# TensorE products without a reader, taken out of the norms of a three-block network

## The chip, the cores and the metric
One Trainium2 chip, one of its cores, one launch. The metric is device time in microseconds. The core has a matrix engine (TensorE, PE in the rows; its weight loads are PEld), VectorE (DVE), ScalarE (ACT), GpSimdE (POOL) and SyncE (SP), which here issues most DMAs. The engines run their own lists of instructions and meet through semaphores.

## The reference, cut to what matters
512 tokens with 1024 channels go through three blocks: a state-space and retention mixer with cross-attention and a gated feed-forward part; a gated convolution and recurrence with 128 experts chosen per token; and a mixer with gating, matrix memory and sparse attention, with a squared-relu feed-forward part. Between the parts stand norms over the 1024 channels, and they are what the change touches:

```python
def _layer_norm(x, g, b):
    mu = jnp.mean(xf, axis=-1, keepdims=True)
    var = jnp.mean(jnp.square(xf - mu), axis=-1, keepdims=True)
    return (xf - mu) * lax.rsqrt(var + EPS) * g + b
...
def third_block(x, c, ...):
        h = rms_norm_3(x, g_norm1[l]) * (1.0 + sc1) + sh1      # behind the second block's own rms norm
        x = x + gt1 * hybrid_mixer_3(h, ...)
        h = rms_norm_3(x, g_norm2[l]) * (1.0 + sc2) + sh2
        x = x + gt2 * (jnp.square(jax.nn.relu(h @ w_mlp1[l])) @ w_mlp2[l])
    return rms_norm_3(x, g_final)
```

## The kernel before, in words
Activations lie with the channel on the partitions: eight tiles of 128 channels x 512 tokens. A linear layer runs over output tiles of 128 channels; a tile takes, for each of the eight input tiles, three matmuls of 128x512 (high part of the weights by high part of the input, high by low, low by high; lines 1008 to 1010, in older form 758 to 760). ScalarE and GpSimdE or VectorE make the two parts of the weights from slabs that SyncE loads. In the rows a matmul on such rounded parts is one record, a matmul in full float32 is two.

A norm needs a sum over channels, that is across partitions, and TensorE makes it. The pieces of work are in `RowNorm`: `means` (line 1175, a 128x128 matrix of ones by the total of the eight tiles), `centre` on VectorE (1180), squares on ScalarE (1186), their sums on TensorE (1233, one row of 512; or 1222, eight matmuls with a single moving column), the root on ScalarE (1256 or 1258), in one form a turn of the row into columns (1240), the reciprocal on VectorE (1263 or 1266), `spreads` (1271: four 128x128 matmuls that bring the factors to all partitions), and then for each tile a scaling on VectorE (1279), the high part on ScalarE (1360, in one norm 1441) and the low part on VectorE (1369 or 1447). The next layer's matmuls wait for these tile by tile.

`Seam` places such a norm between two layers in each engine's list; its `on_pe` is what TensorE runs there. Five norms use the lines that change: the one behind the attention's output layer (`ln2`, line 2756), the one behind the first feed-forward part (`ln3`, 2757, as `WithoutRoot`, which inherits `on_pe`), the two norms in one between the second and the third block (`NormTwice`, 3550), the one ahead of the last feed-forward part (`normed`, 4389) and the final one (`final`, 4390). The norm `ln1` (2424) has a plan of its own that puts its pieces between real output tiles, and no products of this kind.

In between the pieces, `warm(pe, n)` issues n matmuls of a 128x128 matrix of ones with itself, into a PSUM bank that nobody reads at that time (bank 4, in `NormTwice` bank 7). They wait for nothing and signal nothing. The counts are 4, 4 and 6 in `ln2` and `ln3`; 4, 2 and 6 in `normed` and `final`; 3, 6 and 5 in `NormTwice`: 66 in all.

Of the kernel before, what the change touches and what calls it, by code (L numbers as in the profile page):

```python
# [22 lines left out]
P = 128  # L23
# [1261 lines left out]
class Seam:  # L1285
# [12 lines left out]
    def begin(self, split, made, round0):  # L1298
        self.split, self.made, self.round0 = split, (self.s.evac_done, made), round0

    def warm(self, pe, count):
        for _ in range(0 if self.pe_plan else count):
            pe.matmul(self.s.ps[4][:, 0:P], self.s.ones, self.s.ones, start=True, stop=True)  # L1303

    def add_made(self, dve, t):
        if self.first.center:
            self.first.add(dve, t, self.made)
        elif self.first.most_on_dve and t >= 2:
            self.first.add_early_square(dve, t - 1)
# [5 lines left out]
    def sum_up(self, pe, t):  # L1315
        if not self.first.center and not self.first.most_on_dve:
            self.first.column_of_square(pe, t)

    def on_pe(self, pe):
        x, y = self.first, self.second  # L1320
        self.warm(pe, 4)
        if x.center:
            x.means(pe)
            self.warm(pe, 4)
            yield
        if x.sums_on_dve:
            x.column_of_total(pe)
            yield
        elif x.most_on_dve:
            x.columns_of_early_squares(pe)  # L1330
            x.columns_of_last_square(pe)
            yield
        else:
            for t in range(0 if x.center else DT - 2, DT):
                x.column_of_square(pe, t)
                yield
        self.spread(pe, x)
        yield
        if y:
            for t in range(DT):  # L1340
                y.column_of_square(pe, t)
                yield
            self.spread(pe, y)
            yield

    def spread(self, pe, x):
        if x.by_rows:
            x.turn_row(pe)
        else:
            self.warm(pe, 2)  # L1350
        x.spreads(pe)
        self.warm(pe, 6)

    def high(self, act, k):
        x = self.last
# [193 lines left out]
class NormTwice(Seam):  # L1549
# [18 lines left out]
        self.sums = [s.ps[b][:, 0:2 * TT].rearrange("p (j n) -> p j n", n=2) for b in (5, 2)]  # L1568
        self.last = self

    def warm(self, pe, count):
        for _ in range(count):
            pe.matmul(self.s.ps[7][:, 0:P], self.s.ones, self.s.ones, start=True, stop=True)

    def sum_up(self, pe, t):
        pass

# [99 lines left out]
            self.scale(dve, 0, i - 46)  # L1677

    def on_pe(self, pe):
        self.warm(pe, 3)  # L1680
        for t in range(DT):
            self.sum_square(pe, 1, t)
        self.turn_rows(pe, 1)
        self.warm(pe, 6)
        self.spreads(pe, 1)
        self.warm(pe, 5)
        yield

    def shift(self, act, t):
# [108 lines left out]
def first_projection(s):  # L1798
# [79 lines left out]
    def warm(pe):  # L1878
# [8 lines left out]
        part("w_qk", x, store(lambda t: s.qk[:, t, :]), side=first_convs, side_steps=12, side_after="w_xbc"),  # L1887
        part("w_v", x, store_by_token(s.vt, TT), tokens=TT, pe_before=partners, side=rotate, evac_before=silu_beside),
    ], act_start=first_function, sync_first=lambda sync: load_start(s, sync), sync_last=load_rope, pool_end=next_low, pe_start=warm, input_there=input_there)
    s.loaded.passed(16)  # L1890
    s.tables_loaded.passed(16)
# [183 lines left out]
def state_space(s):  # L2075
# [59 lines left out]
    def on_pool(pool):  # L2135
        for _ in range(5):
            yield
        for h in range(SSD_HEADS):
            if h in (2, 12):
                yield  # L2140
            x.weigh_others(pool, h)

    linears_beside(s, [part("w_z", s.x_split, store(lambda t: s.sz[:, t, :]))], Beside(20, 1.0, on_pe, on_act, on_dve, lead=21, pool=on_pool))
    x.passed()

# [57 lines left out]
def retention(s):  # L2203
# [79 lines left out]
    def on_dve(dve):  # L2283
        step = Chain(dve, s.dve_chain)
        dve.wait_ge(s.loaded.sem, s.loaded.at(16))
        for n in range(TT * x.PAIRS):
# [7 lines left out]
            if n in (13, 15):  # L2294
                normalize(dve, step, (13, 15).index(n))

    linears_beside(s, [part("w_g", s.x_split, store(lambda t: s.sg[:, t, :], ACT.Silu))], Beside(18, 1.0, on_pe, on_act, on_dve, load_decay))
    s.loaded.passed(16)
    s.iota_loaded.passed(16)
# [5 lines left out]
def mix(s):  # L2305

    waiting, sq, std = s.view(0, 8), s.view(54, 2), s.arena[0:RET_HEADS, 56 * T:57 * T]
    mean_ready, cen_ready, sq_ready, var_ready, std_ready, spread, applied, high_ready = s.beside_sems[0:8]  # L2310
    y, heads = s.result, RET_HEADS
    mixed = Split(y, 8, s.rounded(8), s.rounded(37))
# [77 lines left out]
    def load_memory(sync):  # L2390
        sync.dma_start(flat(16), s.I["mem"]).then_inc(s.loaded.sem, 16)

    linears_beside(s, [part("w_mixu", Split(lambda k: s.u[:, k, :], 8, s.rounded(58), s.rounded(66)), store(lambda t: waiting[:, t, :]))],
                   Beside(20, 0.95, on_pe, on_act, on_dve, load_memory, lead=8))
    for c, n in ((mean_ready, 8), (cen_ready, 8), (sq_ready, 8), (var_ready, 8), (std_ready, 2), (spread, 8), (applied, 8), (high_ready, 8)):
        c.passed(n)
# [2052 lines left out]
```

## Time and profile before
| | |
|---|---|
| Time, median of 3 runs | 3904.48 us (3903.42 to 3905.22) |
| The profiled execution's own time | 3900.77 us |
| Its span | 3898.7 us |
| Mean granted clock of TensorE | 0.992 |
| TensorE busy | 3550.8 us (91%), 14090 matmul records |
| VectorE, ScalarE, GpSimdE busy | 2322.3, 1502.7, 1279.7 us |
| DMA | 790 MB, mean 203 GB/s |

Busy time says how long an engine had something running; the timeline says what an instruction waited for, and the number in square brackets in a row is the idle time just ahead of it. Granted clock 1.00 is TensorE's higher level (2.4 GHz) and 0.50 the lower one (1.2 GHz). Times in rows count from the start of the span. A row with x8 merges eight records that follow one another, and its duration runs from the first start to the last end; the ends of matmuls are modelled, so a row may overlap the next.

### The profile page before, as it was taken

The numbers are of one execution on the slowest core, as the hardware profiler recorded it, in microseconds if no ns is written. First come the engines' busy times: TensorE is split into PE (matmuls) and PEld (weight loads), VectorE is DVE, ScalarE is ACT, GpSimd is POOL, SyncE is SP. The second block draws the span as 40 slices with busy tenths as digits, with TensorE's granted clock in tenths as the row PEclk, the third lists the DMA queues.
The fourth block names the chain that finished last, engine by engine and source line by source line (L and its number), as shares of the span: only waits on it lengthen the run. The fifth ranks groups of instructions, "written<-read, shape, count | busy, mean of one in ns | idle before, by whom it ended". The sixth has DMA issues, their size and how long they took to land. (4 is left out here: it accounts for less than half of the span.)

```text
span 3898.7 us, 39022 instructions
## 1 busy us (share of the span) xinstructions
PE 3550.8 (91%) x14090; PEld 2366.1 (61%) x14090; DVE 2322.3 (60%) x4229; ACT 1502.7 (39%) x3147; POOL 1279.7 (33%) x858
## 2 busy tenths in 40 slices
PE   9989998999999999998777777778779999999999
PEld 7856686788788778543232232233238666678887
DVE  4763533766856373678877777777751864264161
ACT  1243243543232543244444444445443553333232
POOL 0052352454410014233333333333322222244443
PEclk9999999999999999999999999999999999999999
DMA  3211231225622222899999999999972111122222
GB/s 126 92 65 54 76 130 44 87 97 196 251 87 95 92 89 95 333 422 421 409 422 421 421 402 421 421 398 421 421 300 108 44 70 54 65 87 95 89 98 87
DMA packets 113676, 790.34 MB, mean 203 GB/s; under 512 B 13072, under 2 KB 13264, under 8 KB 21840
## 3 DMA queue, kind: packets, MB, share of 16 engines
q0 software_dynamic: 73728, 536.90, 33.3%
q1 hardware_dynamic: 39760, 250.97, 18.0%
q8 instruction: 113, 1.85, 0.2%
q14 instruction: 75, 0.61, 0.0%
HBM read 785.73 MB, written 2.10 MB: 202 GB/s over the span
## 5 line engine op out<-in xcount | busy, mean ns | idle before, releaser
L3353 PE MATMUL bank<-arena 128*128 128x512 f32 x1984 | 960.6, 611 | 240.7 <-ACT arena L3410 220.7
L3353 PEld LDWEIGHTS bank<-arena 128*128 128x128 f32 x1984 | 348.8, 191 | 816.1 <-issue 796.7
L3463 DVE SCALAR_TENSOR_TENSOR arena<-arena,small,bank 128x1024 f32<-128x1024 f32 x512 | 655.1, 1280 | 301.9 <-DMA arena<-in_experts,arena 298.1
L943 POOL TENSOR_TENSOR weights_lo<-weight_ring,weights_hi 128x1024 fp32r<-128x1024 f32 (+3 forms) x219 | 511.3, 2336 | 939.8 <-ACT weights_hi L1036 939.7
L1008 PE MATMUL bank<-rounded,weights_hi 128*128 128x512 f32 (+1 forms) x2056 | 795.0, 387 | 24.0 <-DVE rounded L1108 7.4
L1009 PE MATMUL bank<-rounded,weights_hi 128*128 128x512 f32 (+1 forms) x2056 | 791.1, 385 | 0.0
L1010 PE MATMUL bank<-rounded,weights_lo 128*128 128x512 f32 (+1 forms) x2056 | 791.1, 385 | 0.0
L3450 POOL DMA_INDIRECT arena<-in_experts,arena x512 | 481.8, 941 | 837.9 <-PE bank L3353 709.1
L1036 ACT ACTIVATE weights_hi<-weight_ring 128x1024 fp32r<-128x1024 f32 (+3 forms) x271 | 270.0, 997 | 703.6 <-PE bank L1010 702.2
L1008 PEld LDWEIGHTS bank<-rounded,weights_hi 128*128 128x128 f32 x2056 | 386.5, 188 | 111.1 <-issue 22.1
L1010 PEld LDWEIGHTS bank<-rounded,weights_lo 128*128 128x128 f32 x2056 | 386.6, 188 | 77.5
L1009 PEld LDWEIGHTS bank<-rounded,weights_hi 128*128 128x128 f32 x2056 | 386.7, 188 | 76.0 <-issue 0.5
L3405 ACT ACTIVATE arena<-arena 128x1 f32<-128x1 f32 x512 | 103.5, 202 | 667.9 <-DVE arena L3463 658.7
L830 POOL TENSOR_TENSOR weights_lo<-weight_ring,weights_hi 128x1024 fp32r<-128x1024 f32 x64 | 154.9, 2420 | 427.3 <-ACT weights_hi L783 427.3
L758 PE MATMUL bank<-rounded,weights_hi 128*128 128x512 f32 x544 | 227.9, 419 | 4.1 <-PEq L510 1.7
L760 PE MATMUL bank<-rounded,weights_lo 128*128 128x512 f32 x544 | 214.4, 394 | 0.0
L759 PE MATMUL bank<-rounded,weights_hi 128*128 128x512 f32 x544 | 214.4, 394 | 0.0
L3410 ACT ACTIVATE arena<-base_tables,arena 128x128 f32<-128x128 f32 x496 | 199.0, 401 | 16.2
L1108 DVE TENSOR_TENSOR rounded<-arena,rounded 128x512 fp32r<-128x512 f32 (+1 forms) x108 | 149.3, 1391 | 37.7 <-ACT rounded L1041 37.5
L3406 ACT ACTIVATE arena<-arena 128x1 f32<-128x1 f32 x512 | 150.8, 295 | 16.7
L783 ACT ACTIVATE weights_hi<-weight_ring 128x1024 fp32r<-128x1024 f32 x64 | 67.7, 1059 | 201.5 <-PE bank L760 197.1
L758 PEld LDWEIGHTS bank<-rounded,weights_hi 128*128 128x128 f32 x544 | 103.1, 190 | 68.6 <-issue 41.4
(482 smaller groups left out, 4572.1 us busy)
## 6 DMA issues: line engine op xcount, KB each, us to landing
arena<-in_w_ada SPq DMA_DIRECT2D x48, 512.0 KB, 8.3
weight_ring<-in_w_up SPq DMA_DIRECT2D x22, 1024.0 KB, 4.8
weight_ring<-in_w_down SPq DMA_DIRECT2D x8, 1408.0 KB, 6.2
weight_ring<-in_w_ga SPq DMA_DIRECT2D x8, 1024.0 KB, 4.8
weight_ring<-in_w_gb SPq DMA_DIRECT2D x8, 1024.0 KB, 4.8
arena<-in_experts,arena POOLq DMA_INDIRECT x512
weight_ring<-in_w_mlp1a SPq DMA_DIRECT2D x8, 1024.0 KB, 4.8
weight_ring<-in_w_mlp2a SPq DMA_DIRECT2D x8, 1024.0 KB, 4.8
```

Of the source, the lines that this page charges most:

```text
L758: pe.matmul(bank(n), hi[:, k, :], x.hi(k), start=first, stop=False)
L759: pe.matmul(bank(n), hi[:, k, :], x.lo(k), start=False, stop=False)
L760: mm = pe.matmul(bank(n), lo[:, k, :], x.hi(k), start=False, stop=last)
L943: eng.tensor_tensor(lo, raw(m), hi.bitcast(F32), ALU.subtract).then_inc(s.lo_made.sem, 1)
L1008: pe.matmul(out, hi[:, k - k0, :], x.hi(k), start=first, stop=False)
L1009: pe.matmul(out, hi[:, k - k0, :], x.lo(k), start=False, stop=False)
L1010: mm = pe.matmul(out, lo[:, k - k0, :], x.hi(k), start=False, stop=last)
L1036: act.activation(hi, raw(m), ACT.Copy).then_inc(s.hi_made.sem, 1)
L3353: mm = pe.matmul(total[:, half * T:(half + 1) * T], diag[:, j, :], rows[:, j, D + half * T:D + (half + 1) * T], start=i % SLOTS == 0, stop ...
L3410: act.activation(diag[:, i % ROWS, :], s.eye, ACT.Copy, scale=weight[:, i:i + 1]).then_inc(s.diag_ready.sem, 1)
L3450: pool.indirect_dma_start(out=rows[:, j, :], out_offset=None, in_=s.I["experts"], in_offset=bass.IndirectOffsetOnAxis(ap=s.expert[:, i:i + ...
L3463: dve.scalar_tensor_tensor(row, row, inverse[:, a:a + 1], tokens(a), ALU.mult, ALU.mult, accum_out=dots[:, i:i + 1]).then_inc(s.dotted.sem, 1)
```

## The change
Both `warm` methods and all calls of them are removed; everything else stays. Line numbers behind the first removed method move up by 4 to 16.

```diff
-    def warm(self, pe, count):
-        for _ in range(0 if self.pe_plan else count):
-            pe.matmul(self.s.ps[4][:, 0:P], self.s.ones, self.s.ones, start=True, stop=True)
...
     def on_pe(self, pe):
         x, y = self.first, self.second
-        self.warm(pe, 4)
         if x.center:
             x.means(pe)
-            self.warm(pe, 4)
             yield
...
     def spread(self, pe, x):
         if x.by_rows:
             x.turn_row(pe)
-        else:
-            self.warm(pe, 2)
         x.spreads(pe)
-        self.warm(pe, 6)
...
-    def warm(self, pe, count):
-        for _ in range(count):
-            pe.matmul(self.s.ps[7][:, 0:P], self.s.ones, self.s.ones, start=True, stop=True)
...
     def on_pe(self, pe):
-        self.warm(pe, 3)
         for t in range(DT):
             self.sum_square(pe, 1, t)
         self.turn_rows(pe, 1)
-        self.warm(pe, 6)
         self.spreads(pe, 1)
-        self.warm(pe, 5)
         yield
```

TensorE's list at `ln2` before, from the last matmul of the layer ahead to the first of the layer behind (`base_tables` holds the ones and the unit matrix, `arena` the activations; here every matmul counts once):

```order
L1010 MATMUL bank<-rounded_3820,weights_lo 128x512
L1303 MATMUL bank<-base_tables 128x128 x4
L1175 MATMUL bank<-arena,base_tables 128x512
L1303 MATMUL bank<-base_tables 128x128 x4
L1233 MATMUL bank<-arena,base_tables 1x512 x8
L1240 MATMUL bank<-base_tables,arena 128x1 x4
L1271 MATMUL bank<-base_tables,small 128x128 x4
L1303 MATMUL bank<-base_tables 128x128 x6
L1008 MATMUL bank<-rounded_3842,weights_hi 128x512
```

The same place after the change:

```order
L1010 MATMUL bank<-rounded_3820,weights_lo 128x512
L1175 MATMUL bank<-arena,base_tables 128x512
L1233 MATMUL bank<-arena,base_tables 1x512 x8
L1240 MATMUL bank<-base_tables,arena 128x1 x4
L1271 MATMUL bank<-base_tables,small 128x128 x4
L1008 MATMUL bank<-rounded_3842,weights_hi 128x512
```

The three runs of products are gone and nothing else has moved. At `NormTwice` TensorE's list read, before:

```order
L3331 MATMUL bank<-base_tables,arena 128x128 x8
L1573 MATMUL bank<-base_tables 128x128 x3
L1592 MATMUL bank<-arena,small 2x128 x8
L1601 MATMUL bank<-base_tables,arena 128x2
L1573 MATMUL bank<-base_tables 128x128 x6
L1636 MATMUL bank<-base_tables,small 128x128 x2
L1573 MATMUL bank<-base_tables 128x128 x5
L1008 MATMUL bank<-rounded_5834,weights_hi 128x512
```

and now, with the lines renumbered (3331 is 3315, 1592 is 1579, 1601 is 1588, 1636 is 1623):

```order
L3315 MATMUL bank<-base_tables,arena 128x128 x8
L1579 MATMUL bank<-arena,small 2x128 x8
L1588 MATMUL bank<-base_tables,arena 128x2
L1623 MATMUL bank<-base_tables,small 128x128 x2
L1008 MATMUL bank<-rounded_5820,weights_hi 128x512
```

Here too only the products are gone. The lists of the other engines hold the same instructions in the same order.

## Rows read from the trace of the kernel before

**Rows 1.** The page's parts 1 and 2: busy time, and TensorE's busy tenths in 40 slices
```profile
PE 3550.8 (91%) x14090; PEld 2366.1 (61%) x14090; DVE 2322.3 (60%) x4229; ACT 1502.7 (39%) x3147; POOL 1279.7 (33%) x858
...
PE   9989998999999999998777777778779999999999
```

**Rows 2.** Groups by line, TensorE: out<-in xcount, busy us, mean ns, idle before
```profile
L1303 PE MATMUL bank<-base_tables 128*128 128x128 f32 x104 | 16.6, 316 | 0.0
...
L1573 PE MATMUL bank<-base_tables 128*128 128x128 f32 x28 | 3.7, 279 | 0.0
```

**Rows 3.** Timeline of TensorE, 679 to 698: start us, us, operation, [idle before <-releaser]
```profile
679.46 1.05 PE L1303 MATMUL bank<-base_tables 128*128 128x128 f32 x8
681.12 1.13 PE L1175 MATMUL bank<-arena,base_tables 128*128 128x512 f32 x2 [0.61 <-DVE arena L1171]
...
683.69 7.28 PE L1233 MATMUL bank<-arena,base_tables 128*1 128x512 f32 x16 [0.55 <-ACT arena L1186]
...
693.06 2.08 PE L1271 MATMUL bank<-base_tables,small 128*128 128x128 f32 x8 [0.28 <-DVE small L1263]
694.93 2.22 PE L1303 MATMUL bank<-base_tables 128*128 128x128 f32 x12
697.61 0.47 PE L1008 MATMUL bank<-rounded,weights_hi 128*128 128x512 f32 x1 [0.46 <-DVE rounded L1369]
```

**Rows 4.** A spread; a window's length, busy us of PE, PEld, DVE, ACT, POOL, PEclk, DMA
```profile
1067.74 1.44 PE L1271 MATMUL bank<-base_tables,small 128*128 128x128 f32 x8 [0.28 <-DVE small L1263]
...
1071.90:1075.30 3.40, 2.82 (x12) 2.17 (x12) 3.15 (x6) 3.17 (x6) 0.00 (x0) 1.00 0.02 5
```

**Rows 5.** Timeline of TensorE, 2904 to 2914
```profile
2904.79 3.56 PE L1592 MATMUL bank<-arena,small 128*2 128x128 f32 x16 [2.16 <-ACT arena L1581]
...
2909.01 1.60 PE L1573 MATMUL bank<-base_tables 128*128 128x128 f32 x12
2910.73 0.71 PE L1636 MATMUL bank<-base_tables,small 128*128 128x128 f32 x4
...
2913.29 0.47 PE L1008 MATMUL bank<-rounded,weights_hi 128*128 128x512 f32 x1 [0.73 <-DVE rounded L1369]
```

**Rows 6.** Timeline of TensorE, 3530 to 3537
```profile
3530.14 1.95 PE L1222 MATMUL bank<-base_tables,arena 128*128 128x1 f32 x16 [0.55 <-DVE arena L1199]
...
3532.65 1.87 PE L1271 MATMUL bank<-base_tables,small 128*128 128x128 f32 x8
...
3536.99 0.47 PE L1008 MATMUL bank<-rounded,weights_hi 128*128 128x512 f32 x1 [0.22 <-DVE rounded L1369]
```

**Rows 7.** Windows laid over the clock's low stretches, and what TensorE did at two
```profile
693.00:696.41 3.41, 3.35 (x15) 3.35 (x16) 1.24 (x3) 0.45 (x1) 2.05 (x1) 0.50 0.00 0
...
3532.90:3536.31 3.41, 3.41 (x18) 3.41 (x18) 1.62 (x3) 1.40 (x3) 2.36 (x1) 0.50 0.80 298
1932.04:1938.87 6.83, 4.47 (x6) 1.89 (x7) 6.59 (x16) 1.84 (x7) 1.04 (x2) 0.50 1.00 393
...
2966.28:2973.11 6.83, 5.76 (x27) 5.76 (x28) 2.85 (x3) 0.49 (x2) 0.00 (x0) 0.50 0.41 156
...
1934.40 2.08 PE L3353 MATMUL bank<-arena 128*128 128x512 f32 x2 [5.80 <-DVE arena L3482]
...
3372.70 4.09 PE L3920 MATMUL bank<-arena,base_tables 4*128 4x512 f32 x8 [1.62 <-DVE arena L3914]
```

**Rows 8.** Timeline of TensorE, dense matmuls at either level
```profile
679.23 0.39 PE L1010 MATMUL bank<-rounded,weights_lo 128*128 128x512 f32 x1
...
3377.31 0.63 PE L759 MATMUL bank<-rounded,weights_hi 128*128 128x512 f32 x1
3377.74 0.63 PE L760 MATMUL bank<-rounded,weights_lo 128*128 128x512 f32 x1
```

**Rows 9.** Timeline of TensorE, the last norm's spreads
```profile
3889.43 1.16 PE L1271 MATMUL bank<-base_tables,small 128*128 128x128 f32 x8
```

**Rows 10.** Timeline of TensorE, a plain wait
```profile
444.62 0.47 PE L1008 MATMUL bank<-rounded,weights_hi 128*128 128x512 f32 x1 [2.54 <-PEq L732]
```

## The prediction
> **What bounds the kernel now.** I read the page's busy shares first: TensorE 91% of the span [rows 1], with a mean granted clock of 0.992 (the table of the profile). TensorE is the bound almost everywhere, so what matters is whether the removed products stand in its way, and what else they do. The second view is their own lines: 104 records of line 1303 and 28 of line 1573, two records to a product, so 52 + 14 = 66 products in five places [rows 2]. By lines they are busy 16.6 and 3.7 us, which looks like a gain of 20 us. The third view, the timeline of each place, says that it isn't.
>
> **Where they lie.** In the norm behind the output projection (line 2756) the first four run from 679.46 for 1.05 us, and the next real matmul starts at 681.12, after 0.61 us more of waiting for VectorE. Four more precede 683.69, again followed by a wait of 0.55 us for ScalarE, and the last six (694.93 to 697.15) are followed by 0.46 us of waiting for VectorE [rows 3]. So removing them frees nothing: the real matmul behind them is late for another reason. The places that need a closer look are those where a real matmul follows without a noted wait: the four spreads at 2910.73 behind six products that end at 2910.61 [rows 5], and those at 3532.65 [rows 6]. Both are spreads that wait for VectorE's reciprocal, and both products end before them with some hundredths of a microsecond to spare. I cost the removed work itself at 0, with at most 0.1 us of gain in each of these two.
>
> **What else they do.** With them in place TensorE's clock falls to its lower level (1.2 GHz, shown as 0.50) once near each of the four norms in the middle of the program: 693.0 to 696.4, 1068.5 to 1071.9 (the windows beside it), 2904.8 to 2908.3, 3532.9 to 3536.3, each 3.41 us long (the first and the last of the four stand in [rows 7]). What TensorE did ahead of them: one-row turns, single-column sums and waits, with few products. What it did inside them: it was busy for 3.35 and 3.41 of 3.41 us in the two rows shown, with spreads and then the useless products. That is the point of this prediction. In the low stretch from 1932.0, in the experts' phase, TensorE went on waiting until 1934.40, and this stretch is 6.83 us long, twice the others. There are four such with waiting in their first part (from 1932.0, 2256.3, 2580.6 and 2966.3), all of 6.83 us; the first and the last stand in the rows [rows 7].
> The Trainium skill, TensorE: Matmul & The Clock Gate, Loop structure matters more than you think, says that a long wait between bursts leaves the next burst cold; by the stretch from 1932.0 the trace agrees. That skill's main page (Trainium Kernel Development and Optimization, Performance Expectations) calls matmul busy time a bad metric: the trace agrees at 3372.70, where TensorE reads as busy for 4.09 us with four-row products and the clock falls inside them, at 3375.88, all the same [rows 7]. By busy time alone the single-column sums of the norms would hold the clock; by this row I take them as not holding it.
>
> **Price of a low stretch.** Dense matmuls start 0.43 us apart at the low level (3377.31, 3377.74) and 0.23 apart at the high one (679.23 and what follows at 679.46) [rows 3, 8]. So 3.41 us of it on dense work loses 3.41 x (1 - 0.23/0.43) = 1.6 us, and 6.83 us loses 3.2. The four spreads take 2.08 us at the low level [rows 3] and 1.16 at the high one [rows 9].
>
> **Place by place.**
> 1. Norm at 679 to 698. The low stretch from 693.0 now holds the spreads (to 695.14) and then nothing until 697.61. I take it that, as from 1932.0, it does not end at 696.4 but 3.4 us or 6.8 us later, at 699.8 or 703.2. Dense work from 697.61 is then slow for 2.2 or 5.6 us: 1.0 or 2.6 us. I take 2.0. New too: between 679.6 and 683.69 TensorE has only the mean's matmul (1.13 us from 681.12, its line 1175). If the clock falls there, the squares' column sums from 683.69 run low. They are paced by columns (7.28/16 = 0.455 us a record [rows 3]), so a stretch costs about 1.7 us and two cost 3.4. Bounds 0 to 3.4; I take 1.0, since a single plain wait of 2.54 us at 444.62 did not bring the clock down [rows 10].
> 2. Norm at 1054 to 1072 (line 2757). The same: the stretch is prolonged over the dense work, 0 to 2.7 us. Here ScalarE is nearly full behind the norm (3.17 of 3.40 us, TensorE 2.82 [rows 4]), so TensorE can catch up on some of it while the eight tiles are handed over. I take 1.2. Mean's part, 0 to 1.7: I take 0.7.
> 3. Two norms at 2901 to 2913 (line 3550). The low stretch to 2908.3 covers sixteen records of the sums and ends as before. From there to 2913.29 TensorE has one short turn of rows (line 1601) and 0.71 us of spreads in 5 us [rows 5]; the six and five products go. A new low stretch then begins near 2911.7 and covers dense work from 2913.3: 1.6 us if 3.4 us long, 5.2 us of dense work and 2.4 if prolonged. Bounds 0.8 to 3.2; I take 2.3.
> 4. Norm at 3528 to 3537. Ahead of 3532.65 stand only single-column sums (1.95 us) [rows 6]; the low stretch holds the spreads and then 2.5 us of waiting, and dense work begins at 3536.99. Bounds 0.8 to 3.2; I take 2.2.
> 5. Last norm, 3885 to the end. No dense work follows, only VectorE's scaling and the stores. In the profiled run the clock was high here; without the products it can fall before the sums or spreads: 0 to 0.9 us on the spreads and up to 0.9 on the sums. I take 0.6.
> Sum: 2.0 + 1.0 + 1.2 + 0.7 + 2.3 + 2.2 + 0.6 = +10.0 us. All low ends: 1.0 + 0 + 0 + 0 + 0.8 + 0.8 + 0 = 2.6; all high ends: 2.6 + 3.4 + 2.7 + 1.7 + 3.2 + 3.2 + 1.8 = 18.6. The profiled execution took 3900.77 us (span 3898.7 and 2.1 around it), 3.7 below the median 3904.48: on it the sum gives 3910.8, on the median 3914.5. TensorE stands at 9 in the slices behind places 1 and 4 [rows 1], so what is lost there isn't won back. Nothing of the DMA queues, ScalarE, VectorE or GpSimdE moves: on TensorE alone 15 runs of products disappear (two of them shown in the order).
>
> **Rivals.**
> A. The low stretches stay as they are: no wait that the change leaves is as long as the 5.80 us ahead of 1934.40 [rows 7], and 2.54 us at 444.62 did nothing [rows 10]. Then the time moves by 0 to +3: 3904 to 3907. Against it: in all four middle norms the clock fell even with the products, so TensorE is at the edge there already. The skill's TensorE page, section Why this matters for your kernels, advises by idle gaps between bursts alone; by that reading this rival holds, since the real matmuls in between cut each gap short.
> B. The clock falls earlier, inside the first wait, and is back by the time of the spreads. Then the spreads run at the high level: 0.9 us at place 1, about 0.3 at place 2 (1.44 instead of 1.16 [rows 4]), 0.7 at place 4, and up to 1.3 for the sums at 2904.79: 3.2 us faster, 3901.3. It decides where the fall comes more than 3.4 us before the spreads and the dense part isn't hit again; that must happen at every place, and the 2.5 us wait before the dense work speaks against it. Even so it stays within what can be measured.
> C. Two falls at most places, one in the first wait and one before the dense work, each prolonged: the high ends, 3904.5 + 16 = about 3920.
> D. The products do stand in TensorE's queue in front of real work and removing them gains their 20 us: 3884. Rows 3 and 5 show the waits behind them, so 1 in 100.
>
> **Chances.** Forecast (one fall per place, prolonged over the dense work) 0.60, A 0.20, B 0.05, C 0.14, D 0.01. A change below 0.2% (7.8 us) can't be told from none for this kernel. Of the forecast about a quarter lies below +7.8, since its low ends sum to less: slower = 0.60 x 0.75 + 0.14 = 0.59, raised to 0.60; faster 0.02; the same 0.38. Range: 3906 leaves out most of A, 3921 holds C. Within the forecast alone 3908 to 3919. When the falls come relative to the kernel may differ from run to run, so its runs may scatter more than the 1.8 us of before.
>
> **What would show it.** In the changed profile: no records of the two product lines; the same starts of the real matmuls relative to each norm's beginning up to the first low stretch; low stretches near all five norms that last 6.8 us or come twice, with dense matmuls (lines 1008 to 1010) 0.43 us apart right behind each norm; mean clock below 0.992 (each 1 us of extra low stretch is 0.5/3900 of it, so about 0.988 to 0.990). Wrong if the dense matmuls behind the norms start 0.23 apart from the first on (A), if the spreads take 1.1 us everywhere and the stretches lie in the waits (B), or if the real matmuls start earlier after each norm's beginning than now (D).

## The result: 14 us slower, and the profile after

| | before | after |
|---|---|---|
| Median | 3904.85 us (8 runs, 3902.45 to 3911.82) | 3919.01 us (8 runs, 3912.74 to 3921.79) |
| Ratio, 95% interval | | 1.0032 [1.0023, 1.0041] |
| The profiled execution's own time | 3900.77 us | 3921.12 us |
| Its span | 3898.7 us | 3919.0 us |
| Mean granted clock of it | 0.992 | 0.983 |

Taking out 66 products that nobody reads made the kernel 14.2 us slower (0.36% by the medians). The page's busy times, after:

```profile
PE 3559.8 (91%) x13958; PEld 2364.9 (60%) x13958; DVE 2322.9 (59%) x4229; ACT 1502.9 (38%) x3147; POOL 1274.5 (33%) x858
...
PE   9989998999999999998777777778779999999998
```

TensorE has 132 matmul records fewer and is busy 9.0 us longer [rows 1]: 20 us of products went, and the rest of its work takes longer. ScalarE, VectorE and GpSimdE do the same work in the same time within 6 us.

The timeline of TensorE in the norm behind the attention's output layer, after (it answers to rows 3; this profile runs 1.4 us ahead of the other up to here, so starts are compared by their distances):

```profile
679.71 1.13 PE L1175 MATMUL bank<-arena,base_tables 128*128 128x512 f32 x2 [1.51 <-DVE arena L1171]
682.28 10.15 PE L1233 MATMUL bank<-arena,base_tables 128*1 128x512 f32 x16 [1.44 <-ACT arena L1186]
693.20 1.05 PE L1240 MATMUL bank<-base_tables,arena 1*128 1x1 f32 x8 [0.77 <-ACT arena L1256]
694.52 1.58 PE L1271 MATMUL bank<-base_tables,small 128*128 128x128 f32 x8 [0.28 <-DVE small L1263]
698.57 0.77 PE L1008 MATMUL bank<-rounded,weights_hi 128*128 128x512 f32 x1 [2.47 <-DVE rounded L1360]
699.14 0.63 PE L1009 MATMUL bank<-rounded,weights_hi 128*128 128x512 f32 x1
699.56 0.63 PE L1010 MATMUL bank<-rounded,weights_lo 128*128 128x512 f32 x1
```

From the mean's matmul to the squares' sums it takes 2.57 us, as before (681.12 to 683.69). But the sixteen records of the sums take 10.15 us instead of 7.28, the spreads start 14.81 us after the mean's matmul instead of 11.94, and the first dense matmuls start 0.57 and 0.42 us apart. The windows over the clock's low stretches in the same profile (length, busy us of PE, PEld, DVE, ACT, POOL, then PEclk):

```profile
681.44:688.28 6.84, 6.00 (x8) 0.76 (x8) 4.31 (x8) 3.11 (x5) 0.29 (x1) 0.50 0.44 153
695.10:701.92 6.82, 4.35 (x14) 3.41 (x13) 5.65 (x9) 2.98 (x5) 1.41 (x1) 0.50 0.00 0
1060.32:1063.74 3.42, 2.82 (x4) 0.42 (x5) 3.42 (x7) 1.77 (x3) 0.00 (x0) 0.50 0.79 278
1073.98:1080.80 6.82, 4.67 (x11) 3.74 (x12) 5.61 (x9) 6.37 (x10) 0.00 (x0) 0.50 0.00 0
2910.34:2927.42 17.08, 11.47 (x36) 8.12 (x37) 8.58 (x22) 9.69 (x22) 5.25 (x3) 0.50 0.18 61
3548.64:3558.88 10.24, 7.76 (x21) 6.25 (x22) 7.99 (x12) 4.96 (x7) 2.35 (x1) 0.50 0.28 104
```

Each row is at 0.50 from end to end. Where the kernel before had one stretch of 3.41 us at each of these norms, there are now two of 6.8 at the first norm (over the sums, and from the spreads on), 3.42 and 6.82 at the second, 17.08 in one piece over the double norm and the work behind it, and 10.24 at the fourth. TensorE at the second norm, at the double norm and at the fourth, after (they answer to rows 4, 5 and 6):

```profile
1060.92 8.65 PE L1233 MATMUL bank<-arena,base_tables 128*1 128x512 f32 x16 [1.45 <-ACT arena L1186]
...
1071.66 1.16 PE L1271 MATMUL bank<-base_tables,small 128*128 128x128 f32 x8 [0.28 <-DVE small L1263]
1076.12 0.77 PE L1008 MATMUL bank<-rounded,weights_hi 128*128 128x512 f32 x1 [3.31 <-DVE rounded L1438]
```

```profile
2912.30 3.57 PE L1579 MATMUL bank<-arena,small 128*2 128x128 f32 x16 [2.90 <-ACT arena L1568]
2916.22 0.58 PE L1588 MATMUL bank<-base_tables,arena 2*128 2x2 f32 x2 [0.35 <-ACT arena L1583]
2918.46 1.23 PE L1623 MATMUL bank<-base_tables,small 128*128 128x128 f32 x4 [1.65 <-DVE small L1617]
2921.34 0.77 PE L1008 MATMUL bank<-rounded,weights_hi 128*128 128x512 f32 x1 [1.65 <-DVE rounded L1360]
2921.90 0.63 PE L1009 MATMUL bank<-rounded,weights_hi 128*128 128x512 f32 x1
```

```profile
3546.14 1.95 PE L1222 MATMUL bank<-base_tables,arena 128*128 128x1 f32 x16 [1.44 <-DVE arena L1199]
3548.65 2.08 PE L1271 MATMUL bank<-base_tables,small 128*128 128x128 f32 x8 [0.57 <-DVE small L1266]
3553.20 0.77 PE L1008 MATMUL bank<-rounded,weights_hi 128*128 128x512 f32 x1 [2.47 <-DVE rounded L1360]
```

In the double norm the spreads take 1.23 us instead of 0.71, and the dense matmuls behind them begin 9.04 us after the sums instead of 8.50, 0.56 us apart. In the fourth, 1.44 us of waiting for VectorE stand ahead of 3546.14, where products and then a wait of 0.55 us lay, and 2.47 ahead of 3553.20. The single-column sums take 1.95 us, as before. At the last norm, with rows 9 beside it:

```profile
3905.81 2.49 PE L1222 MATMUL bank<-base_tables,arena 128*128 128x1 f32 x16 [1.44 <-DVE arena L1199]
3908.86 2.08 PE L1271 MATMUL bank<-base_tables,small 128*128 128x128 f32 x8 [0.56 <-DVE small L1266]
```

Single-column sums 2.49 us instead of 1.95, spreads 2.08 instead of 1.16: the clock fell here too, at 3907.0.

To sum up a place I take the time from one weight load's issue to another that brackets it: a load waits until GpSimdE or VectorE has made the low part of an earlier slab, and that work keeps step with TensorE's. For the first norm these are the first load of w_up and the first of w_down, before:

```profile
661.45 0.33 SPq L960 DMA_DIRECT2D weight_ring<-in_w_up  x1
...
915.16 0.33 SPq L960 DMA_DIRECT2D weight_ring<-in_w_down  x1
```

and after:

```profile
660.05 0.33 SPq L960 DMA_DIRECT2D weight_ring<-in_w_up  x1
...
917.68 0.33 SPq L960 DMA_DIRECT2D weight_ring<-in_w_down  x1
```

253.71 and 257.63 us, so this norm costs 3.9 us. The five places in the same way, from the first issue of each load, in the two profiles, with the prediction's term (loads by the kernel's names: `w2_ax` stands in the rows as `in_w_ax`, `w3_kvc` as `in_w_kvc`):

| Place | bracket | before | after | difference | predicted |
|---|---|---|---|---|---|
| 1, behind attention | w_up, w_down | 253.71 | 257.63 | +3.9 | +3.0 |
| 2, behind feed-forward 1 | w2_ax, w2_ac | 62.90 | 64.67 | +1.8 | +1.9 |
| 3, double norm | w3_kvc, w3_nif | 22.66 | 26.05 | +3.4 | +2.3 |
| 4, ahead of feed-forward 3 | w3_mlp1a, w3_mlp2a | 92.12 | 95.01 | +2.9 | +2.2 |
| 5, last norm | w3_mlp2b, first store | 110.99 | 112.45 | +1.5 | +0.6 |
| Sum | | | | +13.4 | +10.0 |

In the runs below that leave a place unchanged its bracket repeats within 0.4 us, the last norm's within 1.0.

The two profiles lie 20.3 us apart, so 6.9 us of this pair lie elsewhere: 3.2 from `w2_ac` to `w3_kvc`, which is mostly the experts' phase, and 5.1 from `w3_nif` to `w3_mlp1a`, which is that of the sparse attention and the gated memory, less 1.4 ahead of the first norm, with low stretches that the changed code doesn't touch. The pair also flatters the difference: the one execution is 4.1 us below the median of its kernel, the other 2.1 above.

### The profile page after: what moved, and what is told of

The parts are those of the page before. It is cut to its first block and busy times, and to the rows that moved or that the text cites. A ratio compares the mean times of both kernels' runs of the same rounds, so it can differ in the third digit from the quotient of the medians.

```text
span 3919.0 us, 38758 instructions
## 1 busy us (share of the span) xinstructions
PE 3559.8 (91%) x13958; PEld 2364.9 (60%) x13958; DVE 2322.9 (59%) x4229; ACT 1502.9 (38%) x3147; POOL 1274.5 (33%) x858
```

## The experiments

The theory: the products streamed columns through the array in the norms' waits and so held TensorE's clock; without them it falls more often, and the low stretches reach over dense work. The rivals: the products held it merely by keeping TensorE occupied; only one of the runs in each norm matters; the difference is mostly where low stretches happen to fall elsewhere. The experiments change nothing but products that nobody reads, and vary their number, their place and their columns; all of them contract over 128 rows. A ratio is always to the kernel before, run on the same chip.

**The changed kernel again (no edit).**

> The changed kernel again, no edit, beside the kernel before on the same chip. Theory (the removed products held TensorE's clock up in the waits of the five norms): again 10 to 16 us slower than before, ratio 1.0026 to 1.0041; in the profile each of the four middle norms takes 1.5 to 5 us longer from the last dense matmul ahead to a dense matmul well behind. Rival (a good part of the difference is where the clock's low stretches happen to fall elsewhere in the program): ratio under 1.002, and the norms sum to less than 7 us.

3918.22 us, ratio 1.0034 [1.0021, 1.0047]. By its profile the places took 256.71, 62.70, 26.06, 93.38 and 111.08 us: +3.0, -0.2, +3.4, +1.3, +0.1, sum 7.6. So the time repeats, and the ratio decides against the rival; the sum clears its bound of 7 us only just. That each of the four middle norms would take 1.5 to 5 us longer was a miss: the second and the fourth didn't. This execution, 3912.12 us, was the fastest of the five. Where the cost falls changes from run to run, and the second norm shows something more. Its spreads and first dense matmuls, and a window over the low stretch that holds the latter:

```profile
1070.28 1.16 PE L1271 MATMUL bank<-base_tables,small 128*128 128x128 f32 x8 [0.27 <-DVE small L1263]
1074.74 0.76 PE L1008 MATMUL bank<-rounded,weights_hi 128*128 128x512 f32 x1 [3.31 <-DVE rounded L1438]
1075.30 0.63 PE L1009 MATMUL bank<-rounded,weights_hi 128*128 128x512 f32 x1
...
1071.99:1078.82 6.83, 4.08 (x10) 3.24 (x11) 5.62 (x10) 6.04 (x9) 0.28 (x1) 0.50 0.00 0
```

A low stretch of 6.83 us reaches over ten dense matmuls here, as in the first profile, and the bracket is no longer than before (62.70 against 62.90 us). So at this norm the slow dense work is made up for behind it. What cost 1.8 us here in the first profile is the other stretch, over the sums, which is absent in this one.

**Products of one column.**

```diff
-            pe.matmul(self.s.ps[4][:, 0:P], self.s.ones, self.s.ones, start=True, stop=True)
+            pe.matmul(self.s.ps[4][:, 0:1], self.s.ones, self.s.ones[:, 0:1], start=True, stop=True)
```
(and the same in `NormTwice`, with bank 7)

> All 66 products stay in TensorE's queue, each with one moving column instead of 128. By the eight single-column sums of the norms (1.95 us for sixteen records) such a product takes about as long as the full one. Theory (the clock is held by what streams through the array, not by TensorE's being occupied): the time of the changed kernel, +10 to +16 us on before, with low stretches over the dense matmuls behind the norms. Rival (being occupied is enough): the time of before, within 4 us.

3917.2 us, ratio 1.0032 [1.0023, 1.0041]: the changed kernel's time, with all 66 instructions in the queue. TensorE at the first norm in this kernel:

```profile
676.05 0.95 PE L1303 MATMUL bank<-base_tables 128*128 128x1 f32 x8
...
678.68 1.25 PE L1303 MATMUL bank<-base_tables 128*128 128x1 f32 x8
680.29 10.01 PE L1233 MATMUL bank<-arena,base_tables 128*1 128x512 f32 x16 [0.35 <-ACT arena L1186]
...
693.89 2.56 PE L1303 MATMUL bank<-base_tables 128*128 128x1 f32 x12
696.57 0.77 PE L1008 MATMUL bank<-rounded,weights_hi 128*128 128x512 f32 x1
697.13 0.63 PE L1009 MATMUL bank<-rounded,weights_hi 128*128 128x512 f32 x1
```

and the windows over two low stretches there:

```profile
679.18:686.00 6.82, 6.47 (x12) 1.42 (x12) 4.58 (x8) 2.82 (x5) 0.55 (x1) 0.50 0.43 154
692.82:699.66 6.84, 6.72 (x26) 6.03 (x25) 5.39 (x9) 2.82 (x4) 1.57 (x1) 0.50 0.01 2
```

Eight records of one column occupy TensorE for 0.95 and 1.25 us (1.05 with 128 columns in rows 3), and in the two windows it reads as busy for 6.47 of 6.82 and 6.72 of 6.84 us, at 0.50 all the same. The sums take 10.01 us, the dense matmuls start 0.56 us apart. The five places sum to +9.5 us. Occupancy doesn't hold the clock; this decides against the first rival.

**Only the runs behind the spreads stay; only those ahead of them stay.**

```diff
-        self.warm(pe, 4)
...
-            self.warm(pe, 4)
...
-            self.warm(pe, 2)
...
-        self.warm(pe, 3)
...
-        self.warm(pe, 6)
         self.spreads(pe, 1)
```

> Only the last run of products of each norm stays (6, 6, 5, 6, 6: those behind the spreads); those ahead of the spreads are gone. Theory: the stretch that slows the spreads can come earlier, over the single-row sums (+1.7 to +3.4 us at two norms), but a low stretch that holds the spreads ends 3.4 us later instead of 6.8 us, so the dense matmuls behind are mostly spared: +3 to +8 us on before in all. Rival (the runs ahead of the spreads are the ones that count): +10 us or more.

3909.23 us, ratio 1.0012 [1.0003, 1.0021]: +4.4 us, as the theory said. Its low stretches at the first norm:

```profile
679.02:685.84 6.82, 5.63 (x7) 0.75 (x8) 4.66 (x8) 2.74 (x5) 0.63 (x1) 0.50 0.45 154
692.66:696.08 3.42, 3.42 (x18) 3.42 (x18) 1.89 (x3) 1.25 (x2) 1.60 (x1) 0.50 0.00 0
```

The first lies over the sums, ahead of which no products run any more (this norm's bracket 256.05, +2.3); the second, from the spreads on, is filled to 3.42 of 3.42 us with spreads and products and ends after 3.42 us, ahead of the dense work. In the double norm the six products ahead of the spreads are missed:

```profile
2908.97 1.22 PE L1632 MATMUL bank<-base_tables,small 128*128 128x128 f32 x4 [1.65 <-DVE small L1626]
2909.98 2.34 PE L1569 MATMUL bank<-base_tables 128*128 128x128 f32 x10
```

```profile
2901.10:2914.74 13.64, 9.93 (x39) 7.61 (x40) 5.26 (x17) 7.26 (x19) 5.00 (x3) 0.50 0.22 78
```

The low stretch that covers the sums goes on for 13.64 us, in spite of the five products in its last part, and this place costs 2.0 us (24.67). The five places sum to +5.6 us.

```diff
         x.spreads(pe)
-        self.warm(pe, 6)
...
         self.spreads(pe, 1)
-        self.warm(pe, 5)
```

> The counterpart: the last run of products of each norm is gone, those ahead of the spreads stay. Theory: the falls come where they came before, at the spreads, but the stretches reach over the dense matmuls: +1.0 to +2.6 us at each of four norms, +5 to +9 us in all. Rival (the last run is useless since dense work follows anyway): within 2 us of before.

3916.01 us, ratio 1.0025 [1.0016, 1.0034]: +11.1 us, more than the 5 to 9 expected. By its profile the places sum to 1.9 + 0.1 + 0.8 + 2.8 + 0.0 = 5.6 us, within the expectation; most of the rest of that execution's difference lies in brackets without a changed instruction (from w_mixu to w_up 342.1 against 336.1, from phi_k to w_mo 92.5 against 87.1). Whether the eleven runs share this is open. At the second norm a low stretch of 6.83 us lies over the dense matmuls and costs 0.1 us, much as in the second profile of the changed kernel. That the runs of products behind the spreads carry more than those ahead is shown by the times: by means over all runs, and against the 13 of the changed kernel, the 29 products kept behind bring back 8.8 us (plus or minus 2.7, 95%) and the 37 kept ahead 3.0 (plus or minus 3.3). The sums over the places, 5.6 us in both single profiles, don't show it.

**Half the columns.**

```diff
-            pe.matmul(self.s.ps[4][:, 0:P], self.s.ones, self.s.ones, start=True, stop=True)
+            pe.matmul(self.s.ps[4][:, 0:64], self.s.ones, self.s.ones[:, 0:64], start=True, stop=True)
```

> All 66 products with 64 moving columns instead of 128. Theory (streamed columns hold the clock, in proportion): between before and changed kernel, +4 to +10 us. Rival (any full-sized weight load with some columns holds it): within 2 us of before.

3911.74 us, ratio 1.0015 [1.0006, 1.0024]: +6.8 us, as expected. With 128, 64, 1 and no columns in the products the kernel takes 3905, 3912, 3917 and 3919 us: the more columns, the less it loses, though one column can't be told from none. In the profile the places sum to only +0.9 us (the first norm +1.0); that execution, 3907.25 us, is 4.5 below the kernel's median, so where half the columns lose their 6.8 us is not shown.

**Only the double norm's products removed, and only those of the four other norms.**

```diff
-        self.warm(pe, 3)
...
-        self.warm(pe, 6)
         self.spreads(pe, 1)
-        self.warm(pe, 5)
```

> Only the 14 products of the double norm between the second and third block are gone, the other 52 stay. Theory: +2 to +4 us in all, and 3.0 to 3.5 us at that norm in the profile (22.7 us from the load of w3_kvc to that of w3_nif before, 25.1 to 26.1 in the three kernels that lost them or their columns). Rival (this place is part of a long chain through the third block and costs more later): +6 us or more.

3904.9 us, ratio 1.0002 [0.9993, 1.0011], where +2 to +4 was expected: a miss by the time. The place itself did what was expected: 26.02 us against 22.66, with a low stretch as long as in the changed kernel:

```profile
2903.70:2920.78 17.08, 11.42 (x36) 8.14 (x37) 8.64 (x22) 9.74 (x22) 5.29 (x3) 0.50 0.17 62
```

So 3.4 us are there and the medians of 11 and 33 runs, with an interval of 3.5 us to either side, can't show them.

```diff
     def warm(self, pe, count):
-        for _ in range(0 if self.pe_plan else count):
-            pe.matmul(self.s.ps[4][:, 0:P], self.s.ones, self.s.ones, start=True, stop=True)
+        pass
```

> The counterpart of the kernel that lost only the double norm's 14 products: these stay, the 52 of the four other norms are gone. Theory (each norm pays for itself): +8 to +11 us on before, the double norm's stretch from the load of w3_kvc to that of w3_nif back at 22 to 23 us. Rival (the whole effect needs all of them, since where the low stretches fall is shared): under +6 us.

3912.84 us, ratio 1.0022 [1.0013, 1.0030]: +8.9 us; w3_kvc to w3_nif 22.53 us, as before. With the other half that makes 9 to 12 of the 14 us, so each half pays for itself as far as these intervals tell. In the profile the places sum to +9.0 us.

**More products, sized to the waits.**

```diff
-        self.warm(pe, 4)
+        self.warm(pe, 6)
...
-            self.warm(pe, 4)
+            self.warm(pe, 6)
...
+            self.warm(pe, 3)
             x.turn_row(pe)
+            self.warm(pe, 1)
...
-        self.warm(pe, 6)
+        self.warm(pe, 7)
...
-        self.warm(pe, 3)
+        self.warm(pe, 10)
...
-        self.warm(pe, 5)
+        self.warm(pe, 8)
```

> The kernel before with more products, sized to the waits it still has: 6, 6, 7 in the two norms with a row turn and 3 ahead of the turn and 1 behind it; 6, 2, 7 in the two without; 10, 6, 8 in the double norm. Theory: fewer or no low stretches at the norms, the spreads at the higher clock, so 1 to 4 us faster than before (ratio 0.9990 to 0.9997, at the edge of what can be told); the place of each norm in the profile is at or under that of before. Rival (products cost their time in the queue as soon as there are more of them): 1 to 4 us slower.

3903.89 us, ratio 0.9997 [0.9988, 1.0006]: 1.1 us by the medians, no difference that can be told. In the profile the effect is there. TensorE at the first norm:

```profile
681.54 1.50 PE L1303 MATMUL bank<-base_tables 128*128 128x128 f32 x12
...
685.78 7.28 PE L1233 MATMUL bank<-arena,base_tables 128*1 128x512 f32 x16
692.98 0.94 PE L1303 MATMUL bank<-base_tables 128*128 128x128 f32 x6
693.85 1.05 PE L1240 MATMUL bank<-base_tables,arena 1*128 1x1 f32 x8
694.83 0.49 PE L1303 MATMUL bank<-base_tables 128*128 128x128 f32 x2
695.17 1.16 PE L1271 MATMUL bank<-base_tables,small 128*128 128x128 f32 x8
696.17 1.73 PE L1303 MATMUL bank<-base_tables 128*128 128x128 f32 x14
```

and one window over this whole norm:

```profile
681.50:698.00 16.50, 16.11 (x81) 8.40 (x80) 7.94 (x14) 10.03 (x15) 4.71 (x2) 1.00 0.18 65
```

Clock 1.00 throughout, the spreads in 1.16 us; the brackets read 252.80, 62.66, 21.62, 91.87 and 110.98 us, 2.5 us under those of before. There is no low stretch at the first, the second or the double norm. The three products ahead of the turn of the row cost nothing: it starts 8.07 us after the squares' sums, against 8.05 before, and the first dense matmul comes 0.9 us earlier after them, which is what the spreads gain. Why the eleven runs show no more than 1.1 us is not shown; the 2.5 us lie within their interval.

**The same, with 8 products behind the gate turns, and once more.**

```diff
         mm.then_inc(s.gates_turned.sem, 1)
+        for _ in range(8):
+            pe.matmul(s.ps[7][:, 0:P], s.ones, s.ones, start=True, stop=True)
```

> The filled kernel with 8 more products behind the gate turns at the start of the last projection of the third block, where TensorE waits 1.68 us for VectorE's low weights and the clock of before stays low for 6.83 us. Theory: this stretch is halved or gone, 1 to 3 us faster than the filled kernel. Rival (the fall is caused by the 2.74 us of block change ahead, which no product reaches): the same as the filled kernel.

> The filled kernel with the 8 products behind the gate turns again, for a tighter interval. Theory: 2 to 3 us faster than before (ratio 0.9992 to 0.9996) with a mean granted clock of 0.991 against 0.989. Rival (chance): ratio at 1.000, clock the same.

3901.84 us, ratio 0.9996 [0.9987, 1.0005], and again 3903.92 us, ratio 0.9998 [0.9989, 1.0006]. Mean clock over their runs 0.991 and 0.990, against 0.989 before. The stretch behind the gate turns is 3.41 us long in the first profile and gone in the second; but it is 3.41 us long too in four profiles without this edit (both of the changed kernel, half the columns, double norm's removed), so its shortening isn't shown to come from it. The 2 to 3 us expected of the repetition didn't come. These runs have the shortest times of all kernels tried, by 0 to 3 us under before, and can't be called faster.

**All runs together.** Each of the 200 runs of these kernels has a time and a mean granted clock. The time spent at the lower level is 2 x (1 - clock) x time; the mean over a kernel's runs:

| Kernel | runs | at the lower level, us | mean time, us |
|---|---|---|---|
| more products and gate turns | 11, 12 | 70, 75 | 3902.7, 3903.7 |
| more products | 11 | 76 | 3903.8 |
| before | 85 | 85 | 3904.7 |
| double norm's removed | 11 | 92 | 3905.5 |
| only behind the spreads | 11 | 102 | 3909.2 |
| only ahead of the spreads | 11 | 105 | 3915.0 |
| half the columns | 11 | 105 | 3910.2 |
| four norms' removed | 12 | 108 | 3913.6 |
| one column | 12 | 123 | 3916.1 |
| after | 8, 5 | 124, 130 | 3918.2, 3917.6 |

A straight line through all 200 runs rises by 0.28 us for each us at the lower level (correlation 0.89). Within the 85 runs of before alone it is 0.24 (correlation 0.69), so the scatter of one kernel follows the clock too. The change added 39 to 45 us of it, by the line 11 to 13 us. Only the kernel without products behind the spreads lies well off, 4 us above the line; that its low stretches fall on dense work rather than in waits would fit, and is not shown.

The profiles also tell how much lies outside the five places. Of each profiled execution I take its time less that of before (3900.77 us) less its sum over the places. The eleven values run from -4.5 to +15.2 us, the more products' kernels among them with +3.7, -1.9 and +7.1, and their mean is 3.8 us. The execution of before was itself 4.1 us under its kernel's median. So on average nothing is left outside the places, while a single profile can be off by 10 us.

## Why the prediction came out, and where its terms were off

- **The removed work frees nothing: right.** Where the removed runs stood TensorE now waits about that much longer (1.51 us ahead of 679.71 where 0.61 stood, 2.47 ahead of 698.57 where 0.46 stood). Rival D's 20 us don't exist.
- **A low stretch that contains the wait behind the spreads is prolonged over the dense work: right**, at places 1 to 4 in the changed profile. The run without products ahead shows it from the other side: with the products behind the spreads kept, the stretch of the first norm ends after 3.42 us.
- **Price, 1.6 us for 3.41 us on dense work: borne out in the rate, and in time only where nothing makes up for it.** Dense matmuls start 0.42 us apart in it. At the fourth norm 3.41 us more of low stretch cost 1.3 us (second profile of the changed kernel) and 6.83 more cost 2.9. At the second norm a stretch of 6.83 us cost -0.2 and 0.1 us, where 1.2 stood in the sum. ScalarE is nearly full there (6.04 of 6.83 us), which was the prediction's own reason for a low term; that this is the cause is argued, not tested.
- **Place 2 came out by luck.** Its +1.8 us against 1.9 are made of a dense part that cost next to nothing instead of 1.2 and sums that cost 1.4 instead of 0.7.
- **"One fall per place" was the likeliest case; the profile after shows rival C at two places.** At places 1 and 2 the clock fell already over the squares' sums. The terms taken there for the mean's part, 1.0 and 0.7 us, were too small: the sums alone took 10.15 - 7.28 = 2.9 and 8.65 - 7.28 = 1.4 us more. I had leaned on a single wait of 2.54 us without a fall [rows 10], where the right comparison is two waits of 1.5 us with one matmul between them. In the second profile of the changed kernel the first norm has 3.41 us there and the second none, so what happens is a mixture of the forecast and C, and the measured 3919 us lie nearer to C's 3920 than to the forecast's 3914.5. (C's +16 us are less than the high ends that it names, which sum to 18.6.)
- **Place 3 was taken too small** (2.3, measured 3.4, 3.4 and, alone, 3.4 us): the stretch over the sums doesn't end at the sums, as I took it to, but runs on for 17.08 us. **Places 4 and 5** measured 2.9 and 1.3, and 1.5 and 0.1, around the terms of 2.2 and 0.6.
- **Total: 3914.5 predicted, 3919.0 measured**, +14.2 against +10.0. The sum was right in kind and 4 us short. Which terms are short by that much the profiles don't settle: the places sum to 13.4 us in one and 7.6 in the other.
- **The mean clock was to be 0.988 to 0.990: a miss.** It was 0.983 in the profile and 0.984 over the 13 runs. The 0.992 that it was reckoned from was a good execution (0.989 over 85 runs), and the change added 39 to 45 us at the lower level, more than the 16 to 31 us that 0.988 to 0.990 stand for. That the time moved by only 14 us is because a us at the lower level cost 0.28 us on average, not the 0.47 of dense work.
- **Rivals A and B: out.** The dense matmuls behind the norms start 0.57 and then 0.42 us apart, from the first on, and the spreads took 1.58, 1.16 and 2.08 us at places 1, 2 and 4.
- **The scatter was foretold in direction only**: runs of the changed kernel spread over 9 us. Those of before, of which three had shown 1.8 us, spread over 9 too, and over 14 in all 85.
- The Trainium skill's advice by idle gaps between bursts alone (TensorE: Matmul & The Clock Gate, Why this matters for your kernels) would have given rival A. The measurement decides against it: at the first norm no gap is longer than 2.47 us, and the clock fell twice. (One gap reaches 3.31 us, at the second norm.)
- The prediction called busy time a bad metric and took the trace to agree. What the Trainium skill says there (Trainium Kernel Development and Optimization, Performance Expectations) is about how close a kernel is to its roofline. That busy time doesn't tell the clock either rests on the rows at 3372.70 and on the run with one column, not on that page.

Open: where half the columns lose their time, why the kernel without products behind the spreads is 11 us slower by its runs while its places sum to 5.6, and why the slow dense work at the second norm costs so little.

## What to carry to other kernels

Before removing an instruction whose result nobody reads, ask what it does to the clock: here 66 products worth 20 us of busy time, all inside waits, saved 14 us. In this kernel such products had to stream many columns and lie inside waits, and those right ahead of dense work were worth most; placed there they cost nothing, and more of them gained nothing that the times could show. And where a cost is a few us in 3900, sum it by brackets around the place in the profile as well as by the total, since the total moves by more from run to run.

## What the runs showed of the hardware

- Being occupied doesn't hold TensorE's clock: in the kernel with one-column products it read as busy for 6.72 of 6.84 us at the lower level, and that kernel was as slow as the one without products (3917.2 and 3918.2 us in one comparison). Weight loads don't hold it either: in the same 6.84 us they read as busy for 6.03.
- Half the columns gave about half the effect: +6.8 us, between 0 with 128 and +12.3 with one.
- Columns alone are not the measure either. In the kernel before, the four products at 3372.70 (eight records) stream 512 columns each, but contract over four rows and not 128, and the clock fell within them, at 3375.88. A window over the time just ahead of the fall:

```profile
3372.47:3375.88 3.41, 3.18 (x8) 1.40 (x8) 2.08 (x4) 3.26 (x4) 0.56 (x1) 1.00 0.00 0
```

  TensorE read as busy for 3.18 of the 3.41 us. Products with full columns and few rows in the norms' waits would tell whether rows count as columns do; no run here has them.
- Low stretches lasted 3.4, 6.8, 10.2, 13.6 and 17.1 us. At the norms of the changed kernel the longest were those in which waits and short matmuls kept following each other: of the 17.1 us only the last 6.1 hold dense matmuls.
- The squares' sums onto one row ran at half speed in a low stretch although they need a single column of weights: 10.15 us instead of 7.28.
